# Seven-product weight sums: one set per up-projection iteration behind the up tile's first splits, and four sets in the mixer

## What is computed

```python
n1 = rmsnorm(x, norm_mix_g)
q, k, v, o, i_f, x_r, g_r = split(n1 @ w_in)          # w_in: 2048 x 6152
h_m = mlstm_chunkwise(q, k, v, i_f) * sigmoid(o)      # 4 heads of 256, per-head norm
h_r = rglru(x_r) * gelu(g_r)                          # conv of width 4, gates, scan
x = x + concat(h_m, h_r) @ w_out                      # 2048 x 2048
gate, up = split(rmsnorm(x, norm_ffn_g) @ w_up)       # w_up: 2048 x 11264
x = x + (silu(causal_dwconv(gate, width 3)) * up) @ w_down   # w_down: 5632 x 2048
return rmsnorm(x, norm_final_g)
```

## Time and profile before

| | us |
|---|---|
| median of 3 runs | 1151.64 |
| lowest, highest | 1147.49, 1152.27 |
| the profiled execution, its own time | 1149.87 |
| its span (first to last instruction) | 1148.1 |
| mean granted TensorE clock | 0.991 |

### The profile page before, as it was taken

One profiled execution on the slowest core, in us unless ns is written; L12 is line 12 of the kernel. 1 busy time (PEld: TensorE's weight loads), 2 busy tenths in 40 slices (PEclk: granted clock), 3 DMA queues, 4 the chain that ended last, 5 costly groups with the idle time before them and its releaser, 6 DMA issues.

```text
span 1148.1 us, 16882 instructions
## 1 busy us (share of the span) xinstructions
PE 1115.7 (97%) x5950; PEld 957.5 (83%) x5950; DVE 856.9 (75%) x1124; ACT 616.8 (54%) x794; POOL 48.5 (4%) x44
## 2 busy tenths in 40 slices
PE   9999999999999999799998899989999999999996
PEld 8888888888888888688887788877888888888885
DVE  6677585775957676778777777777688797897887
ACT  7665474554847543444344344443444476767774
POOL 0100000000000000000000000000000000000001
PEclk9999999999999999999999999999999999999998
DMA  8756657565556587799977999768998898869982
GB/s 257 233 169 197 170 150 220 154 200 170 163 183 213 156 297 250 256 284 293 316 240 230 294 292 319 255 219 273 308 286 303 285 317 310 295 241 314 340 293 95
DMA packets 183845, 282.37 MB, mean 246 GB/s; under 512 B 8908, under 2 KB 151504, under 8 KB 180608
## 3 DMA queue, kind: packets, MB, share of 16 engines
q1 hardware_dynamic: 182784, 279.61, 75.1%
q0 software_dynamic: 448, 1.78, 0.5%
q10 hardware_dynamic: 576, 0.53, 0.1%
HBM read 254.62 MB, written 27.27 MB: 246 GB/s over the span
## 4 chain that ended last, share of the span: by engine, by line
PE 73%; DVE 11%; DMA 8%; ACT 3%; issue 3%; SPq 2%; ACTq 0%; DVEq 0%
PE ps L1430 28%; PE ps L1565 16%; PE ps L1432 14%; PE ps L1614 9%; DMA raw<-w_up_dram 7%; DVE w L838 4%; ACT w L510 2%; PE ps L1427 2%; DVE fc L1261 2%; DVE s_raw L1294 1%; PE ps L1428 1%; DVE fc L1257 1%; DVE fg L1251 1%; DVE s_raw L1297 1%; DVE fg L849 1%
## 5 line engine op out<-in xcount | busy, mean ns | idle before, releaser
L1430 PE MATMUL ps<-xT,w 128*128 128x512 f32 x2048 | 727.7, 400 | 19.1 <-DVE w L838 19.1
L838 DVE TENSOR_TENSOR w<-raw,w 128x1024 fp32r<-128x1024 f32 x340 | 416.0, 1238 | 217.1 <-ACT w L510 216.3
L1432 PE MATMUL ps<-xT,w 128*128 128x256 f32 x2048 | 574.9, 281 | 0.0
L510 ACT ACTIVATE w<-raw 128x1024 fp32r<-128x1024 f32 (+3 forms) x373 | 386.6, 1053 | 330.2 <-PE ps L1432 179.5
L1430 PEld LDWEIGHTS ps<-xT,w 128*128 128x128 f32 x2048 | 387.3, 189 | 114.3 <-DVE w L838 21.6
L1432 PEld LDWEIGHTS ps<-xT,w 128*128 128x128 f32 x2048 | 388.9, 190 | 0.3
L1565 PE MATMUL ps<-w,aT 128*128 128x512 f32 x864 | 198.1, 389 | 0.0
L1565 PEld LDWEIGHTS ps<-w,aT 128*128 128x128 f32 x864 | 161.8, 188 | 33.7
L1614 PE MATMUL ps<-s_w,s_act 128*128 128x512 f32 x336 | 79.5, 391 | 0.0
L1614 PEld LDWEIGHTS ps<-s_w,s_act 128*128 128x128 f32 x336 | 63.1, 188 | 13.7
L510 ACT ACTIVATE fs<-fc 128x512 f32<-128x512 f32 x22 | 13.9, 632 | 110.6 <-DVE fc L1261 110.6
(11 more groups left out here) (178 smaller groups left out, 635.1 us busy)
## 6 DMA issues: line engine op xcount, KB each, us to landing
raw<-w_up_dram SPq DMA_DIRECT2D x176, 512.0 KB, 6.1
raw<-w_in_dram SPq DMA_DIRECT2D x92, 512.0 KB, 3.9
s_raw<-w_down_dram SPq DMA_DIRECT2D x64, 512.0 KB, 7.0
sums<-s_raw SPq DMA_DIRECT2D x48, 512.0 KB, 7.7
raw<-w_down_dram SPq DMA_DIRECT2D x48, 512.0 KB, 5.9
raw<-w_out_dram SPq DMA_DIRECT2D x32, 512.0 KB, 4.3
s_raw<-sums SPq DMA_DIRECT2D x16, 1024.0 KB, 7.4
raw<-sums SPq DMA_DIRECT2D x8, 1024.0 KB, 7.6
```

Source lines behind the costliest of these rows:

```text
L510: return sc.activation(out_, in_, fn, **kw)
L838: v.tensor_tensor(w[:, s, :, 1, :], raw[:, s, :].rearrange("p (c n) -> p c n", c=CH), w[:, s, :, 0, :], ALU.subtract).then_inc(lo_ready, 1)
L1430: mm(full, w[:, s, c, 0, cut], xT[:, kt, :, :].rearrange("p a n -> p (a n)"), start=kt == 0, stop=False)
L1432: ins = mm(rest, w[:, s, c, 1, cut], xT[:, kt, 0, :], start=False, stop=kt == KT - 1)
```

## The change

- The list SUMS_AT goes. 20 of the 24 sets are made in iterations 0 to 19 of the up projection, one in each, at a fixed place: SyncE issues the two stores of the set before and the two loads of this set together behind the raw load of gate unit 3; VectorE does the first instruction behind the split of up unit 4 (ahead of it a wait for the stores of the set before and for the rows), the other two behind the split of up unit 5.
- Four sets (half 1, i = 2, runs 0 to 3) are made in the mixer, one in each head: the loads stand behind the raw loads of group XR, VectorE's three instructions behind the splits of units 0, 1 and 2 of group GR, the stores behind the raw loads of the next head's group V (for the last head, behind the first half of the output projection's loads). VectorE waits for the stores at the end of a head, ScalarE before its squares in the output projection (they write `xn`), SyncE once for "std1" ahead of the heads.

The arithmetic of a set, its bytes and the number of sets are the same.

```diff
-UP_UNITS = 2 * RING * (UP_ITERS - 1)
-SUMS_AT = [1 + (UP_UNITS - 9) * t // (2 * PAIRS - 1) for t in range(2 * PAIRS)]
-SUMS_STORE = 6
+MIX_SUMS = 1
+MIX_SETS = MIX_SUMS * (H - 1) + 1
...
+        def mixer_pair(i, m):
+
+            return 1, i, RUN_PAIRS - 1
+
+        up_pairs = [(half, run, i) for half in range(2) for run in range(RUNS) for i in range(RUN_PAIRS)]
+        for i in range(H):
+            for m in range(MIX_SUMS if i < H - 1 else 1):
+                up_pairs.remove(mixer_pair(i, m))
...
+            def load_for_sums(half, run, i):
+
+                k = run * RUN_TILES + (RING + 2 * i)
+                for row in range(2):
+                    src = down_rows[bass.ds(k + row, 1), :, half * HALF:(half + 1) * HALF].rearrange("k p n -> p (k n)")
+                    sp.dma_start(s_raw[:, row * HALF:(row + 1) * HALF], src).then_inc(t_raw_landed, 16)
+
+            def store_sums(t, half, run, i):
+
+                dst = [sums_dram[bass.ds(sums_place(half, run, i), 1), :, part * HALF:(part + 1) * HALF].rearrange("t p n -> p (t n)") for part in range(2)]
+                sp.wait_ge(t_summed, t * T_SUMS + T_SUMS)
+                for part in range(2):
+                    sp.dma_start(dst[part], s_raw[:, (2 + part) * HALF:(3 + part) * HALF]).then_inc(t_stored, 16)
...
                 for g, col in enumerate((COL_O, COL_XR, COL_GR)):
                     load_group(g0 + g, in_v, i * COLS + col)
+                    if g == 1:
+                        load_for_sums(*mixer_pair(i, 0))
...
                     for g, col in enumerate((COL_V, COL_Q, COL_K)):
                         load_group(g0 + 3 + g, in_v, i * COLS + (col + COLS))
+                        if g == 0:
+                            store_sums(i * MIX_SUMS, *mixer_pair(i, 0))
...
+            after(sp, A0, "std1")
             with sp.Fori(0, H - 1) as i:
                 load_head(i, False)
...
+                if half == 0:
+                    store_sums(MIX_SETS - 1, *mixer_pair(H - 1, 0))
...
-                    def sums_of(s, unit=(2 * (j - 1) + g) * RING):
-                        here = unit + s
-                        for part in range(2):
-                            if here + 1 - part in SUMS_AT:
-                                load_for_sums(SUMS_AT.index(here + 1 - part), part)
-                            if here - SUMS_STORE - part in SUMS_AT:
-                                store_sums(SUMS_AT.index(here - SUMS_STORE - part), part)
+                    def sums_of(s, n=j - 1, first=g == 0):
+                        if first and s == RING - 1:
+                            if 0 < n <= len(up_pairs):
+                                store_sums(MIX_SETS + n - 1, *up_pairs[n - 1])
+                            if n < len(up_pairs):
+                                load_for_sums(*up_pairs[n])
...
                     warm_sqrt(A2)
+                    act_e.wait_ge(t_stored, 32 * MIX_SETS)
...
+            def weight_sum(t, n):
+
+                if n == 0:
+                    dve.wait_ge(t_raw_landed, t * 32 + 32)
+                    v.tensor_tensor(t_out[:, 0:2, :], t_raw[:, 0:1, :].to_broadcast([P, 2, BANK]), t_raw[:, 1:3, :], ALU.subtract).then_inc(t_summed, 1)
+                else:
+                    dve.wait_ge(t_summed, t * T_SUMS + n)
+                    v.tensor_tensor(t_out[:, n + 1, :], t_raw[:, n + 1, :], t_out[:, 2 * n - 2, :], ALU.subtract).then_inc(t_summed, 1)
...
-                split_units(g0 + 2)
+                for s in range(RING):
+                    split_units(g0 + 2, [s])
+                    if s < T_SUMS:
+                        weight_sum(i * MIX_SUMS, s)
...
+                    dve.wait_ge(t_stored, i * (32 * MIX_SUMS) + 32)
...
-                def split_and_sum(n, group, unit=2 * j * RING):
+                def split_and_sum(n, group):
                     for s in range(RING):
                         split_units(group, [s])
-                        here = unit + n * RING + s
-                        for part in range(2):
-                            if here - 1 - part in SUMS_AT:
-                                weight_sums(SUMS_AT.index(here - 1 - part), part == 0)
+                        if n == 1 and s < 2 and j < len(up_pairs):
+                            for m in range(1) if s == 0 else range(1, T_SUMS):
+                                if s == 0:
+                                    dve.wait_ge(t_stored, 32 * (MIX_SETS + j))
+                                weight_sum(MIX_SETS + j, m)
```

More of the change, by code:

```diff
@@ L382, in _, with sums_place @@
             down_rows = w_down.rearrange("(k p) n -> k p n", p=P)
[L384 to L396, removed]
+            def sums_place(half, run, i):
+                return run * (2 * RUN_PAIRS) + (half * RUN_PAIRS + i)
+            def load_for_sums(half, run, i):
[8 more added lines that the diff above has]
+                    sp.dma_start(dst[part], s_raw[:, (2 + part) * HALF:(3 + part) * HALF]).then_inc(t_stored, 16)
             def load_pair(half, run, i):
@@ L405, in load_pair @@
                 lower = down_rows[bass.ds(k + 1, 1), :, cols:cols + HALF].rearrange("k p n -> p (k n)")
-                sums = sums_dram[bass.ds(run * (2 * RUN_PAIRS) + (half * RUN_PAIRS + i), 1)].rearrange("t p n -> p (t n)")
+                sums = sums_dram[bass.ds(sums_place(half, run, i), 1)].rearrange("t p n -> p (t n)")
                 if i == 1:
@@ L467, in _ @@
                 for g in range(2):
-                    def sums_of(s, unit=(2 * (j - 1) + g) * RING):
-                        here = unit + s
-                        for part in range(2):
-                            if here + 1 - part in SUMS_AT:
-                                load_for_sums(SUMS_AT.index(here + 1 - part), part)
-                            if here - SUMS_STORE - part in SUMS_AT:
-                                store_sums(SUMS_AT.index(here - SUMS_STORE - part), part)
+                    def sums_of(s, n=j - 1, first=g == 0):
[4 more added lines that the diff above has]
+                                load_for_sums(*up_pairs[n])
                     load_up(j, g, sums_of)
+            if len(up_pairs) == UP_ITERS - 1:
+                store_sums(2 * PAIRS - 1, *up_pairs[-1])
             load_body(G_DOWN, w_down, 0, 0)
@@ L1011, in _ @@
             after(dve, V0, "pads")
+            t_raw, t_out = (s_raw[:, n * 2 * HALF:(n + 1) * 2 * HALF].rearrange("p (m n) -> p m n", m=SUMS) for n in range(2))
+            def weight_sum(t, n):
[5 more added lines that the diff above has]
+                    v.tensor_tensor(t_out[:, n + 1, :], t_raw[:, n + 1, :], t_out[:, 2 * n - 2, :], ALU.subtract).then_inc(t_summed, 1)
             def head(i, last):
@@ L1284, in row_sums @@
                 v.tensor_tensor(block(S4), block(A12), block(S2), ALU.subtract).then_inc(s_summed, 1)
[L1286 to L1299, removed]
             n_up = G_UP - NOT_BANKED
```

## The result

| | before, us | changed, us |
|---|---|---|
| median of 4 runs each, taken in turn | 1151.91 | 1117.48 |
| lowest, highest | 1147.49, 1152.27 | 1117.33, 1117.71 |
| the profiled execution, its own time | 1149.87 | 1117.37 |
| its span | 1148.1 | 1115.6 |

The ratio is 0.971 with a 95% interval of 0.9686 to 0.9734: faster, 2.5 us under the forecast of 1120 and inside the range. The 23 further runs of the kernel before that stand beside the experiments have medians of 1149.0 to 1149.5, so the gain is nearer to 32 us than to the 34.4 of this table.

The account below looks back on a forecast made before the run. TensorE, busy 97% of the span, was taken as the bound, with everything to win in the up projection. Profiled 1149.9 - 32.2 gain + 1.8 to the median = 1119.5, forecast 1120; range 1112 to 1141.

Parts of the forecast that it names:

- The stretch: Up projection, 21 iterations: 466.2 us for 498.4, gain 32.2: waits 19.1, half-clock stretches some 6.5, slower pace about 6.6.
- The transfers: Up projection: 2.0 us latency plus 1.54 us per transfer; unit 4's load lands at T + 11.2, needed T + 11.8.
- T: Moment in an up-projection iteration when the split of unit 7 ends; the burst of sum transfers goes out then.
- VectorE: Up projection: 2.6 us of sums fit 3.8 us idle; units 5, 6, 7 late by 0.6, 0.4, 0; 1.2 left.
- The wait for t_stored: Up projection, ahead of the sum: stores land by T + 6.6, loads T + 9.7, sum starts T + 15.1; costs nothing.
- SyncE: Up projection: the burst's issues take at worst 5.7 us, under the 6.8 until unit 4's load; nothing queued is late.
- Mixer: Mixer: four sets of 2.6 us fit VectorE's idle time and cost 0; with no fit 10.4 us.
- Places 5 and 6: Kernel before, up projection: sum loads at these iteration places push later raw loads back; TensorE's waits follow exactly these sets.
- 1, the slower pace: Up projection: no waits, but iterations stay at 22.6 us; gain 23.8, total 1128; chance 0.25.
- 2, waits in each iteration: Up projection: each of the 20 iterations with a set loses 0.5 to 1 us, total 1130 to 1140; chance 0.13.
- 3: Up projection: total traffic crowds, not its place; mean loss of 1.5 us an iteration stays, about 1150; chance 0.08.
- 4, slower than before: Up projection: a transfer takes over 2.0 us, transfers become the bound, TensorE waits in each iteration; 1167; chance 0.07.

Follow-up runs that it names:

- experiment 7: Three kernels: changed kernel with VectorE's sums cut to 8 columns, 1118.55; with stores two units earlier, 1117.75; with transfers behind raw load 4 cut to 128 columns, 1117.73.
- experiment 4: Two kernels from the one before, all sets but the first: VectorE's sums cut to 8 columns, 1136.04; second, sum transfers cut to 128 columns, 1118.17.
- experiment 7, last column: Changed kernel with the sum transfers one raw load later, behind up unit 4's, and cut from 1024 to 128 columns: 1117.73 us.
- stores earlier: Changed kernel with the two stores behind the raw load of gate unit 1 in place of unit 3, loads kept: 1117.75 us.
- experiment 5: Changed kernel with the mixer's four sets left out (loads, sums, stores and waits): 1117.73 us, beside 1117.49 for the changed kernel.
- Experiments 3: Changed kernel with its 20 up-projection sets placed by a sliding list as before, the mixer's four kept: 1136.84 us, ratio 0.9893 to the kernel before.
- experiment 2: Changed kernel with all three VectorE sums behind up unit 7's split, directly ahead of the convolution, transfers kept: 1141.14 us, ratio 0.9933 to the kernel before.
- experiment 6: Changed kernel with 6.2 us of extra VectorE work ahead of the convolution in one iteration, to stop TensorE once: 1131.59 us.
- small sums: Changed kernel with VectorE's up-projection sums cut to 8 columns from the second set on, transfers kept: 1118.55 us.

## Why the prediction was right, step by step

- *The stretch.* 21 x 22.2 = 466.2 was forecast. The start of the down projection moved by 32.7 us for a forecast of 32.2. All three terms went: the waits of the earlier trace rows, the stretches at half clock, the slower pace. That the pace would be the quicker one, which the prediction gave 0.47 against 0.25, has held in every profiled execution without a wait: the changed kernel twice, the one without the mixer's sets, the three new ones of experiment 7, and the second of experiment 4.
- *The forecast 1120 against 1117.48.* By the profiled executions' own times the gain is 32.5 for 32.2, and 0.5 was rounding. The other 1.8 were my step from the profiled execution to the median: it was laid on the new kernel too, whose profiled execution (1117.37) lies on its median. That step rested on a median of three runs, 1151.64; the 23 runs beside the experiments lie at 1149.0 to 1149.5 in the median, and the profiled execution (1149.87) was no lower than those. The kernel before does spread more (1147.1 to 1154.3) than the changed one (1117.3 to 1118.3); that its stops differ from run to run is likely, but only one of its executions has a trace.
- *The transfers.* The price of one held: from 567.34 to 575.27 five of them land in 7.93 us, 1.59 each, for 1.54. The window there:

```profile
567.34:575.27 7.93, 7.93 (x47) 6.94 (x46) 5.59 (x6) 2.73 (x4) 0.00 (x0) 1.00 1.01 346
```

  The term that was mis-sized is the first: "a lone raw load lands in 3.5 us" was put in for raw load 3, the shortest of the four in the earlier trace rows. Behind other raw loads and with no burst it takes 4.52 (experiment 7, last column), with the burst behind it 5.70, and 5.97 in this example. With this term right the sum is T + 5.97 + 7.93 = T + 13.9 instead of T + 11.2. The "0.6 us to spare" turned into a lateness of 2.1 us (T + 13.9 against T + 11.8), ScalarE starts within 0.11 us of the landing in every one of the 19 iterations, and "unit 4's load landing within about 5 us" was wrong (6.1 to 7.8). The price per transfer, 1.54 us, was right to 0.05; the fit that the prediction sets against it is given in the Trainium skill ("DMA: Bandwidth & Descriptors", section "Anatomy of one DMA") for DMAs that GpSimd issues, and all of these are issued by SyncE.
- *VectorE.* Lateness of 0.6, 0.4 and 0 us for units 5, 6 and 7 was forecast. Measured from T, the splits of units 4 to 7 start 2.2, 1.7, 1.4 and 0 us later (medians) than in the version "stores earlier" of experiment 7, since unit 4 itself is late. (From the end of their rounding the last three start after 0.81, 1.72 and 0.08 us.) So the 1.2 us that were to be left on VectorE are gone in most iterations. What carried the forecast is reserve behind this step. At unit 0 the prediction had 2.1 us, read where the pace was the slower one; at the quicker pace it is 1.72 with no unit late, and 1.7 in the median here, 0.80 at least. The larger reserve the prediction did not name: TensorE takes unit 4 only 3.3 us after its split in the median and 2.4 at least (5.8 with no unit late), so a late unit 4 is no wait of TensorE. The prediction did not count on it, so that the time came out although the step of the transfers failed is in part luck. Experiment 2 shows the price where VectorE's 2.6 us stand behind the last of this reserve.
- *The wait for t_stored.* Stores at T + 7.2 and T + 8.6 (forecast by 6.6), loads at T + 9.5 and T + 12.4 (9.7), sum at T + 16.3. It never held VectorE, whose only waits with an entry in the stretch are for ScalarE's rounding:

```profile
DVE w L859 <- ACT w L530: 96.3, 69, 3.6
```

- *SyncE.* The burst's issues end at 564.98, T + 3.6, ahead of the bound of 5.7 and of the next raw load.
- *Mixer.* Forecast 0, measured within 1 us (experiment 5).
- *Places 5 and 6 as the cause in the kernel before.* Experiments 3 and 4 agree, with two corrections. The seven waits follow these sets, but for the last and shortest (0.9 us), which stands behind a set of place 4. And the prediction counted the sums in the loop as a second cost of its own; alone they cost nothing there (1118.17), and add 13 us only on top of late raw loads. In every iteration, all three right ahead of the convolution, they do cost by themselves (experiment 2).
- *Rivals.* 1, the slower pace, did not come, but is what a wait can bring (experiment 6, 14.1 us). 2, waits in each iteration, is what experiment 2 has. 3 is half right: the traffic does crowd, but its place decides, since the changed kernel moves 280 GB/s in this stretch without a wait, where the kernel before moved 279. 4, slower than before, needs no transfer of 2.0 us: one raw load's difference in place gives 1180.42 at a DMA share of 0.79. The rival had the wrong mechanism; its price of 1167 was even too low for what one step to the side does.

## What to carry over

Place extra transfers where the next load of the stream is longest away, and check it with a landing time of a load that has the same neighbours, not with the shortest landing of the trace. One step to the side can cost more than all that was to be won (63 us lost, where the whole gain is 32). Once TensorE is busy throughout, better spacing gives only reserve; but the stops here cost more than their length (14.1 us for one of 4.6 in experiment 6, 32 for the 19 of the kernel before), so reserve is worth having.

## What was not expected of the hardware

- Two steady paces of the same matmuls at a granted clock of 1.00, 22.2 and 22.6 us an iteration, changed in the up projection of these traces only across a wait of TensorE. Why a wait brings one or the other stays open: of the 20 waits of experiment 2, all between 0.49 and 0.76 us, 14 were followed by the slower pace and 6 by the quicker.
- SyncE's issue of a 512 KB transfer mostly takes 0.33 to 0.6 us, but can take 1.3 to 1.9 us behind a close series of others. The count outstanding alone does not set it: in the up projection of the changed kernel the median is 0.38 us with four outstanding (98 issues, the longest 1.77) and 1.70 with five (13 issues, one of them the last load of the burst above). With sums transfers of 64 KB those take at most 0.51 us.
- A load is slowed by transfers that are issued after it: raw load 3 takes 4.52 us with nothing large behind it, and 5.70 with four transfers behind it (5.82 where the spacing ahead of it is even, too: experiment 7, small sums).
- For 5 us, from 565 to 570, the core moves 382 GB/s; over the whole burst it is 346. The Trainium skill ("DMA: Bandwidth & Descriptors", section "Bandwidth") has about 358 GB/s per core binding on the HBM side, which the prediction weighed. The same section gives about that share for two cores that stream from one HBM domain, and more, up to 425, as measured for a core whose neighbour is idle. This kernel runs on one core, and its 382 GB/s agree with the second:

```profile
565.00:570.00 5.00, 5.00 (x31) 4.39 (x30) 3.35 (x4) 3.48 (x4) 1.30 (x1) 1.00 1.02 382
```
